# Reordering one DMA queue and moving the mLSTM set-up, its exponentials and its output gate in a hybrid decoder step on one core

## The reference, cut to what matters

```python
z = h @ w_in                                   # columns shared out to three mixers
# A) GLA: S_t = diag(a_t) S_{t-1} + k_t^T v_t, o_t = q_t S_t, chunk by chunk
# B) NSA attention: compressed, selected and window branch; the sample tokens
#    read cache_nsa_kv[page_table], compressed by a small MLP
# C) mLSTM, chunk by chunk, with a carried matrix state C:
dmat = where(causal, fcum[t] - fcum[s] + i[s], -inf)
qk   = einsum('bhtd,bhsd->bhts', q, k) * exp(dmat - m_t)
num  = einsum('bhts,bhse->bhte', qk, v) + w_state * einsum('bhtd,bhde->bhte', q, C)
C    = w_carry * C + einsum('bhs,bhsd,bhse->bhde', w_last, k, v)
o_m  = sigmoid(mo) * (rmsnorm(h_m, g) + ml_skip * u_act)   # output gate and skip
x = x + concat([o_g, o_n, o_m]) @ w_out
x = x + relu(rmsnorm(x) @ w_up)**2 @ w_down
```

## Time and profile before

| what | us |
|---|---|
| median of 3 runs | 1873.37 (1870.58 to 1886.39) |
| the profiled execution | 1873.04 |
| its span | 1871.0 (PE busy 1743.5) |
| `gla_and_gather` | 660.4 to 877.6 (217.2; PE busy 194.7, granted clock 0.94) |
| `mlstm_prompt` | 877.6 to 932.3 (54.7; PE busy 41.7, granted clock 0.67) |
| `decode_steps` | 932.3 to 965.5 (33.2; PE busy 22.2) |
| `decode_tail` | 965.5 to 1014.3 (48.8; PE busy 23.9) |
| `mix_and_mixer` | 1014.3 to 1871.0 (856.7; PE busy 837.7, granted clock 0.99) |

### The profile page before, as it was taken

How to read it: one execution, slowest core, us unless ns; L and a number is a source line. 1 busy time by engine, 2 the same in 40 slices (tenths; PEclk the granted TensorE clock), 3 DMA queues, 4 the chain that set the end, 5 groups by cost and what they waited for, 6 DMA issues and landing times. The chain is left out here.

```text
span 1871.0 us, 32344 instructions
## 1 busy us (share of the span) xinstructions
PE 1743.5 (93%) x12895; PEld 1620.8 (87%) x12895; DVE 1052.0 (56%) x1876; ACT 632.0 (34%) x1141; POOL 175.2 (9%) x205
## 2 busy tenths in 40 slices
PE   6999999979999978998865899999999999999998
PEld 6999999968888766786732899999999999999998
DVE  6372683258777755665566666444444444444445
ACT  6523331047555544443342344111112111111111
POOL 1000000022222242223111100000000000000000
PEclk7999999969999989999676999999999999999999
DMA  7741264250000165665566562111111111111102
GB/s 187 115 106 34 64 174 147 91 158 24 14 2 1 46 217 180 230 233 185 119 124 224 155 190 69 46 45 45 45 45 45 45 45 45 45 45 45 45 23 91
DMA packets 180898, 177.18 MB, mean 95 GB/s; under 512 B 51564, under 2 KB 163268, under 8 KB 177140
## 3 DMA queue, kind: packets, MB, share of 16 engines
q1 hardware_dynamic: 173924, 132.92, 25.2%
q0 software_dynamic: 2304, 33.56, 4.7%
q10 hardware_dynamic: 4560, 9.18, 1.8%
HBM read 139.60 MB, written 40.23 MB: 96 GB/s over the span
## 5 line engine op out<-in xcount | busy, mean ns | idle before, releaser
L59 PE MATMUL pm<-hH,wuH 128*128 128x344 f32 x768 | 246.3, 321 | 0.0
L61 PE MATMUL pm<-hH,wuL 128*128 128x344 f32 x768 | 245.0, 319 | 0.0
L60 PE MATMUL pm<-hL,wuH 128*128 128x344 f32 x768 | 245.0, 319 | 0.0
L59 PE MATMUL pm<-hidH,weights 128*128 128x344 f32 x720 | 230.7, 320 | 0.0
L60 PE MATMUL pm<-hidL,weights 128*128 128x344 f32 x720 | 230.2, 320 | 0.0
L61 PE MATMUL pm<-hidH,weights 128*128 128x344 f32 x720 | 230.0, 319 | 0.0
L59 PE MATMUL pz<-hH,winH 128*128 128x344 f32 x600 | 200.1, 334 | 1.6 <-DVE hL L845 1.6
L60 PE MATMUL pz<-hL,winH 128*128 128x344 f32 x600 | 194.1, 323 | 0.0
L61 PE MATMUL pz<-hH,winL 128*128 128x344 f32 x600 | 194.0, 323 | 0.0
L3302 DVE SCALAR_TENSOR_TENSOR act<-pm,onat 128x344 f32<-128x344 f32 x96 | 49.3, 515 | 239.7 <-PE pm L61 239.3
L3313 DVE TENSOR_TENSOR onat<-pm,onat 128x344 f32<-128x344 f32 x256 | 128.9, 513 | 68.9 <-PE pm L61 68.9
(11 more groups left out here) (610 smaller groups left out, 3501.1 us busy)
## 6 DMA issues: line engine op xcount, KB each, us to landing
uact<-in_w_up_dram SPq DMA_DIRECT2D x15, 1024.0 KB, 6.9
hs<-in_w_down_dram SPq DMA_DIRECT2D x15, 1024.0 KB
raw<-in_w_in_dram SPq DMA_DIRECT2D x24, 512.0 KB, 3.8
hold<-vS_scratch SPq DMA_DIRECT2D x8, 1024.0 KB, 14.4
wo<-in_w_out_dram SPq DMA_DIRECT2D x12, 512.0 KB
act<-in_w_out_dram SPq DMA_DIRECT2D x12, 512.0 KB, 5.2
zT_scratch<-zb ACTq DMA_DIRECT2D x8, 516.0 KB, 2.6
hold<-in_x_prompt_dram SPq DMA_DIRECT2D x8, 512.0 KB, 3.8
```

The source lines that it names most:

```text
L59: nc.tensor.matmul(out, wH, mH, start=start and k == 0, stop=False)
L60: nc.tensor.matmul(out, wH, mL, start=False, stop=False)
L61: last = nc.tensor.matmul(out, wL, mH, start=False, stop=stop and k == n - 1)
```

## The change

In `attend_prompt` a few buffers are allocated in another order, and SP's loads of queries and keys are reordered (the wait for the late part of z stands before keys part 4, after four query tiles and not three).

In `gla_and_gather` SP's queue goes by halves, and the small loads are spread over iterations 1 to 5. After the last gather POOL makes the masks of the next stage in a buffer that the page rows no longer need, and ACT and DVE make the rounded copies and the low part of the gates at n = 9 and n = 11 of the last iteration.

In `mlstm_prompt` the set-up is gone, `scores` is split into `decays` and `products`, `decays` runs two chunks ahead, the Sigmoid of `mo` stands after the exponential of chunk 3, and POOL's product and the warming Exp are gone.

In `decode_steps` SP loads `gains`, `skip` and `g2` after the store of `mo`. In `decode_tail` ACT multiplies `uact` by `skip`. In `mix_and_mixer` the sum with `uact` comes first and the product with `mo` after it, in one piece.

```diff
@@ attend_prompt, SP @@
-                for n in range(NQS - 1):
+                for n in range(len(KEY_PARTS) - 2):
                     load_q(n)
                     load_keys(n)
-                for n in range(NQS - 1, len(KEY_PARTS) - 1):
-                    load_keys(n)
+                for n in range(len(KEY_PARTS) - 2, NQS):
+                    load_q(n)
                 sp.wait_ge(keep["late_z"], 16 * 3)
-                for n in range(NQS - 1, TQ):
+                load_keys(len(KEY_PARTS) - 2)
+                for n in range(NQS, TQ):
                     load_q(n)
@@ gla_and_gather, SP (keep_values(s, half): the wait for the gather and the vS store;
   store_scores(s, half): the wait for the copied scores and four stores) @@
                     if 1 <= s < NCH - 1:
                         sp.wait_ge(og_done, s)
                         load_z(s + 1)
-                    for half in range(2):
-                        ... (the vS store)
-                    for half in range(2):
-                        ... (four stores of the scores)
-                    if s == 1:
-                        load_small_steps(sp, io, at, small_in)
+                    keep_values(s, 0)
+                    if s:
+                        store_scores(s - 1, 1)
+                    keep_values(s, 1)
+                    store_scores(s, 0)
+                    if 1 <= s <= 5:
+                        load_small_steps(sp, io, at, small_in, s - 1)
+                store_scores(NS - 1, 1)
@@ load_small_steps: part 0 = qkd and the four loads of head 0, parts 1 to 3 = the four
   loads of heads 1 to 3, part 4 = the two loads of gbd @@
@@ gla_and_gather, POOL, after the last gather @@
+                pool.wait_ge(f_done, NFILL * (NS - 1) + 6)
+                pool.wait_ge(v_stored[0], 16 * NS)
+                nc.gpsimd.memset(spread[:, :, :], 0.0).then_inc(pages_over, 1)
...
+                nc.gpsimd.affine_select(out=maskT[:, :, :], ...).then_inc(ml_masks, 1)
@@ gla_and_gather, ACT @@
+                        if n == 9 and it == NCH - 1:
+                            act.wait_ge(pages_over, 1)
+                            nc.scalar.activation(gates_r[:, :], R[0:64, :], ACT.Copy).then_inc(gates_high, 1)
+                            nc.scalar.activation(ident_m[:, :], ident[:, :], ACT.Copy)
+                        if n == 11 and it == NCH - 1:
+                            act.wait_ge(ml_spread, 1)
+                            nc.scalar.activation(spread_r[:, :, :], spread[:, :, :], ACT.Copy)
+                            act.wait_ge(ml_masks, 1)
+                            nc.scalar.activation(maskT_r[:, :, :], maskT[:, :, :], ACT.Copy)
@@ gla_and_gather, DVE @@
+                        if n == 11 and it == NCH - 1:
+                            dve.wait_ge(gates_high, 1)
+                            nc.vector.tensor_tensor(gates_r[32:36, :], R[0:4, :], gates_r[0:4, :].bitcast(F32), ALU.subtract)
@@ mlstm_prompt, POOL @@
-                (the memsets and affine_selects of sel127, spread, maskT)
                 constants_of_steps(nc, pool, keep, at, laid)
-                pool.wait_ge(mo_ready, 1)
-                for hp in range(HP):
-                    nc.gpsimd.tensor_tensor(uact[:, hp, :], uact[:, hp, :], at["mo"][:, hp * TT:(hp + 1) * TT], ALU.mult)
@@ mlstm_prompt, PE (decays = L2186 to L2192, products = L2193 to L2200) @@
-                scores(0)
+                decays(0)
+                products(0)
+                nc.tensor.matmul(pc[:, 0:P], sel127[:, :], ...).then_inc(wc_done, 1)
+                decays(1)
                 for c in range(NCH):
                     ... (pd(c))
                     if c + 1 < NCH:
-                        scores(c + 1)
+                        products(c + 1)
+                    if c + 2 < NCH:
+                        decays(c + 2)
                     ... (pn(c), pa(c))
@@ mlstm_prompt, ACT @@
                 for c in range(NCH):
+                    if c == 1:
+                        act.wait_ge(wc_done, 1)
+                        ... (the copy wcb, before at the stage's start)
                     ... (four Exp)
-                act.wait_ge(mo_in, 16)
-                nc.scalar.activation(at["mo"], at["mo"], ACT.Sigmoid).then_inc(mo_ready, 1)
-                nc.scalar.activation(warm[:, :], keep["eps"][0:1, :], ACT.Exp)
+                    if c == 3:
+                        act.wait_ge(mo_in, 16)
+                        nc.scalar.activation(at["mo"], at["mo"], ACT.Sigmoid)
@@ decode_steps, SP, after the store of mo (removed from decode_tail's SP) @@
+                (two loads of gains for each half, one of skip, one of g2)
@@ decode_tail, ACT, after the squares sqh @@
+                act.wait_ge(gains_in, 16 * 6)
+                for hp in range(HP):
+                    nc.scalar.activation(keep["uact"][:, hp, :], keep["uact"][:, hp, :], ACT.Copy, scale=skip[:, hp:hp + 1])
@@ mix_and_mixer, DVE, build(i) @@
-                    last = nc.vector.scalar_tensor_tensor(out=tmp[:, :, 0:n], in0=mls, scalar=gains[:, 1:2], in1=mo[:, :, at],
-                                                          op0=ALU.mult, op1=ALU.mult)
+                    last = nc.vector.scalar_tensor_tensor(out=tmp[:, :, 0:n], in0=mls, scalar=gains[:, 1:2], in1=uact[:, :, at],
+                                                          op0=ALU.mult, op1=ALU.add)
                     nc.vector.drain()
-                    for hp in range(HP):
-                        last = nc.vector.scalar_tensor_tensor(out=mixc[:, i % 2, 2 + hp, 0:n], in0=uact[:, hp, at], scalar=skip[:, hp:hp + 1],
-                                                              in1=tmp[:, hp, 0:n], op0=ALU.mult, op1=ALU.add)
-                    last.then_inc(mixc_ready, 1)
+                    nc.vector.tensor_tensor(mixc[:, i % 2, 2:4, 0:n], tmp[:, :, 0:n], mo[:, :, at], ALU.mult).then_inc(mixc_ready, 1)
```

More of the change, by code:

```diff
@@ L1608, in gla_and_gather @@
         sem = semaphores(nc, ctx, "gla", (at["gathered0"],))
+        with ExitStack() as after:
+            ml = lambda n, s, d=F32: after.enter_context(nc.sbuf_tensor(n, s, d))
+            at.update({"sel127": ml("sel127", [P, P]), "maskT_r": ml("maskT_r", [P, 4, P], F32R), "ident_m": ml("ident_m", [P, P], F32R),
+                       "spread_r": ml("spread_r", [64, 4, P], F32R), "gates_r": ml("gates_r", [64, T], F32R)})
+            spread, maskT = ml("spread", [64, 4, P]), ml("maskT", [P, 4, P])
+        sel127, maskT_r, ident_m, spread_r, gates_r = (at[n] for n in ("sel127", "maskT_r", "ident_m", "spread_r", "gates_r"))
+        R = keep["rows"]
+        sb("pages_kept", [P, 8 * 512])
         spare = keep["rows_nat"][:, :, :].rearrange("p i c -> p (i c)")
@@ L1670, in load_w1, with keep_values, store_scores @@
                                      io["w1S"].rearrange("p (j r w e) -> p j r w e", j=2, r=16, w=2)[:, j, at, :, :]).then_inc(w_in[half], 16)
+                def keep_values(s, half):
+                    sp.wait_ge(gathered[half], 16 * (s + 1))
+                    sp.dma_start(io["vS"][s, :, half * 8:half * 8 + 8, :].rearrange("p r (h d) -> p r h d", h=2),
+                                 kv[half][:, :, 3, :, :]).then_inc(v_stored[half], 16)
+                def store_scores(s, half):
+                    sp.wait_ge(sc_kept, 2 * s + half + 1)
+                    for u in range(4):
+                        sp.dma_start(sS[s * 8:s * 8 + 8, half, :, u, :], sst[32 * u:32 * u + 8, half, :].rearrange("h (f p) -> h f p", f=2)
+                                     ).then_inc(sc_stored[half], 16)
                 load_z(0)
@@ L2043, in place_small_steps, with load_small_steps @@
             "gf": sb("gfd", [P, HP, NS]), "gb": sb("gbd", [P, 2, HP])}
-def load_small_steps(sp, io, at, loads):
+def load_small_steps(sp, io, at, loads, part):
     zT = io["zT"]
-    sp.dma_start(at["qk"][:, :, :], zT[GQ:GQ + 4 * P, T:TT].rearrange("(j p) s -> p j s", p=P)).then_inc(loads, 16)
-    for h in range(4):
+    if part == 0:
+        sp.dma_start(at["qk"][:, :, :], zT[GQ:GQ + 4 * P, T:TT].rearrange("(j p) s -> p j s", p=P)).then_inc(loads, 16)
+    for h in ((part,) if part < 4 else ()):
         rws, hp = slice((h % 2) * 64, (h % 2) * 64 + 64), h // 2
@@ L2055, in load_small_steps @@
         sp.dma_start(at["gf"][rws, hp, :], zT[MF + h:MF + h + 1, T:TT].broadcast_to([64, NS])).then_inc(loads, 16)
-    for h2 in range(2):
+    for h2 in (range(2) if part == 4 else ()):
         sp.dma_start(at["gb"][h2 * 64:h2 * 64 + 64, :, :],
@@ L2192, in scores, with products @@
                     last.then_inc(pw_done, 1)
+                def products(c):
                     if c:
@@ L2304, in decode_steps @@
         mt, C, stored = at["mt"], at["C"], at["sample_out"]
+        gains, skip, g2, gains_in = keep["gains"], keep["skip"], keep["g2"], at["gains_in"]
         qbd, qbm = sb("qbd", [P, HP, NS, 2]), sb("qbm", [P, HP, NS, 2])
@@ L2345, in _ @@
```

(10 more changed lines are left out.)

82 lines of the change are left out of this document (24 added, 58 removed).

## The result

The changed kernel takes 1861.55 us in the median of 13 runs (1857.01 to 1869.50); the kernel before, timed beside it, 1875.04 (13 runs). The ratio is 0.9928, with a 95% interval of 0.9911 to 0.9945: 0.7% faster. The forecast was 1847 us, in a range of 1835 to 1860, so the gain is about half of what was forecast and the time lies 1.6 us above the range.

What follows compares the result with a forecast made beforehand. PE, busy 1,744 of 1,871 us, was taken as the bound, so only its idle or half-rate time could earn; −14.4 + 6.0 + 0.4 − 16.7 − 1.0 = −25.7 gave 1847 us, range 1835 to 1860.

Steps and rivals of the forecast that it cites:

- The −14.4 for the burst: GLA stage: spreading SP's 19 small loads removes one long iteration's idle time and half-rate work, −14.4 us.
- The +6.0 for the small groups: GLA stage: four groups of small loads each delay a gather by 1.5 us, +6.0 us (bounds 0 and 12.4).
- The DVE subtraction (+0.4): GLA stage: DVE's 1.21 us subtraction stands before the last merges and costs between 0 and 1.2, taken as +0.4 us.
- start to first `pdm`: mLSTM stage: `decays(0)` begins at once, without waiting for masks, 4.2 us to the first `pdm`, −5.9 us.
- seven intervals: mLSTM stage: from first to eighth `pdm`, two intervals of 6.2 and five of 3.45, 29.7 for 36.8, −7.1 us.
- from the eighth `pdm` to the end: mLSTM stage: POOL's tail goes, −3.8 us, and the Sigmoid among the exponentials costs +0.1 us.
- how many intervals run at half rate?: mLSTM stage: PE's clock falls at the barrier and two intervals run at half rate, between none and four.
- The Sigmoid in the middle (+0.1): mLSTM stage: Sigmoid and two table loads, 4.5 us between exponentials, which ACT catches up; 0 to 3, taken as +0.1 us.
- Two chunks ahead: mLSTM stage: earlier input to the exponential removes PE's wait at full rate, an interval of 3.45 in place of 3.83 us.
- decode_steps and decode_tail (0): Decode stages: SP's six moved issues (3.6 us) and ACT's two products with `skip` fall into idle time, 0.
- The mix (−1.0): `mix_and_mixer`: one product replaces two pieces, −0.46 us for each build, bounds 0 and −4.1, taken as −1.0 us.
- the clock's staying down: Rival, mLSTM stage: the clock stays down as long as before, four intervals, +5.5 us, time 1853; chance 0.20.

Runs made afterwards that it cites:

- e4: The kernel before with only the 19 small loads of the GLA stage spread over iterations 1 to 5, behind the score stores: 1864.61 us, ratio 0.9927.
- e5: The changed kernel with `decays(c+2)` put directly before `products(c+1)`, still two chunks ahead: 1857.83 us, ratio 0.9892.
- e12: The changed kernel itself once more, unaltered: 1859.50 us, ratio 0.9922.
- e1: The changed kernel with seven transposes of the identity after PE's last GLA output, in front of the barrier: 1853.73 us, ratio 0.9885.
- e3: The changed kernel with all 19 small loads in one run in GLA iteration 1 again: 1869.97 us, ratio 0.9961.
- e7: The changed kernel, its order kept, with 13 transposes of the identity around PE's last GLA output: 1847.07 us, ratio 0.9810.
- e2: The changed kernel with `decays(c+1)` directly before `products(c+1)`, one chunk ahead as in the kernel before: 1852.30 us, ratio 0.9866.
- e9: The changed kernel with 13 transposes around the last GLA output and `decays(c+1)` directly before `products(c+1)`, one chunk ahead: 1854.43 us, ratio 0.9896.
- e10: The program of e6 with the Sigmoid of `mo` moved after the last exponential: 1846.29 us, ratio 0.9861.
- e11: The program of e6 once more, in more rounds: 1847.89 us, ratio 0.9872.
- e15: The program of e5 once more: 1853.87 us, ratio 0.9883.
- e8: The changed kernel with one more matmul of 512 columns, result unused, in every mLSTM chunk but the first: 1849.17 us, ratio 0.9865.
- e14: The changed kernel with `decays(c+2)` directly before `products(c+1)` and an added matmul in every chunk but the first: 1855.48 us, ratio 0.9901.
- e16: The program of e8 once more: 1856.75 us, ratio 0.9901.
- e6: The changed kernel with `decays(c+2)` directly before `products(c+1)` and 13 transposes around PE's last GLA output: 1837.34 us, ratio 0.9801.
- e13: The program of e6 with an added matmul in every chunk but the first and two more before the first `pdm`: 1844.10 us, ratio 0.9831.

## Why the prediction was wrong, point by point

**The GLA stage: right in what goes, wrong in what comes.** The −14.4 for the burst is what was measured (−14.0 with everything). The +6.0 for the small groups (1.5 us for each of four) was mis-sized: it is 0 in the changed kernel. The place was right, beside the gather of half 0; the price was not. I took it from a gather in the middle of the burst (14.3 us to landing), and here the loads begin behind the gather, which then lands after 8.9 to 9.1 us, 0.3 to 0.5 us over the 8.6 that I had reckoned with and within the 2.6 to spare. The price that I had in mind is paid in e4, where the loads begin ahead of a gather: its groups cost 14.4 − 5.7 = 8.7 us, in a place that I did not name (the gather of half 1). The Trainium skill ("DMA: Bandwidth & Descriptors", section "Issuing engines are not separate DMA queues") has all transfers interleave on the same 16 engines, by which the upper bound, 12.4 us, had been weighed; e4's landings of 13.4 to 14.5 us agree with it. The upper bound that I drew from it does not hold in the changed kernel, where the landings are 8.9 to 9.1 us.

**The DVE subtraction (+0.4):** not visible; the stage is 14.0 shorter where −14.4 alone would be 0.4 more, but its length in the eight traces with this stage's code unchanged runs from 202.5 to 203.9.

**The mLSTM stage: here it failed.** By its terms, from the two timelines:

| term | forecast | measured |
|---|---|---|
| start to first `pdm` | −5.9 | −5.1 (4.9 us in place of 10.1) |
| seven intervals | −7.1 | +8.1 (44.9 in place of 36.8) |
| from the eighth `pdm` to the end | −3.7 | −2.9 (5.0 in place of 7.9) |

The step that failed is "how many intervals run at half rate?": I took two, with four as the upper bound, and all seven did. The bound was four because the kernel before had four, and I argued that more work from the start could only bring the clock back sooner. The runs show otherwise. The second step that failed is smaller and was in the diff to be seen: I priced an interval at half rate as unchanged, 6.2 us, "running `decays` two ahead is worth nothing there", but the new neighbours cost 0.5 us in each of the six intervals that still hold a `decays`, 2.9 us together; the seventh is 1.3 us shorter than 6.2, for the `decays` that went in front. e5, with both neighbours put back, has 6.17 us. I had weighed each matmul by its own duration and not by its neighbours.

What holds the clock down? Of the traces in which it fell at the start of the stage, the changed order without added work has five (the changed kernel, e12, e1, e3, e7), and in none did it come back within 49 us of the stage's start, when the recurrence was in its last chunk or over. With `decays` directly before `products` there are eight, with the masks made early or late: it came back after 18 to 36 us in seven (before, e2, e5, e9, e10, e11, e15), and only after 55 us in one, e4 (its stage: 59.9 us). With a matmul added to each chunk it came back after 27, 19 and 19 us in all three (e8, e14, e16). From the first `pdm` to the clock's return PE is busy without a gap in all of these stretches, so "busy" does not tell them apart. Nor do the transfers of the stage: the clock came back while the DMA engines were at a share of 1.4 (e5, 886 to 896), and stayed at 0.50 long after they had gone quiet (0.01 in the changed kernel from 895 to 917). That the changed order delays the return is therefore well supported in the traces, and that one more matmul in each chunk brings the clock back in the same order is what e8 and e16 show in one execution each. How it is decided stays open, and so does why one program (e6 and e11, or e4 beside the kernel before) goes one way in one execution and another in the next. The share of executions in which the clock comes back isn't known: only the traced ones show it, and the medians of e5, e14, e15 and e16 (1854 to 1858) lie nearer the changed kernel's (1860 to 1862) than their traces would suggest.

**The Sigmoid in the middle (+0.1):** right, by e6's trace, as long as `decays` is two chunks ahead (e2's pause of 2.16 us). The Trainium skill ("ScalarE: Activation LUTs", section "What ACT_TABLE_LOAD costs") has a drain of some 1.4 us besides the load of 1.28 at each change of table; here e6's load begins at 876.35 and the Sigmoid at 877.64, so no drain is seen.

**Two chunks ahead:** 3.45 us forecast at full rate, 3.31 measured in e6, with no wait of PE. In the changed kernel it earned nothing, since no interval ran at full rate.

**decode_steps and decode_tail (0):** −0.6 and +1.2. In decode_tail the read of `win_rows` from `sS_scratch` held DVE 2.80 us where it had been 0.85:

```profile
963.98 2.28 DVE L2799 TENSOR_REDUCE bm<-win_rows 64x32 f32<-64x2048 f32 x1 [2.80 <-DMA win_rows<-sS_scratch]
```

It starts 12.6 us after the stage's start, before 10.4. That the six loads moved ahead of decode_steps' stores are the cause wasn't tried, and the difference itself is within the scatter: the same code took 47.1 to 50.6 us for this stage in the other traces. The two products by `skip` on ACT took 2.2 us of idle time, as forecast (5.91 us of idle time remain of 7.79).

**The mix (−1.0):** the one product takes 0.43 us in the chain of work, where the two pieces took 0.62 to 0.70:

```profile
1033.32 0.43 DVE act L3268
```

The stage as a whole took between 851.6 and 858.6 us in the traces of this study and 856.7 before, so a microsecond can't be found in it.

**The chances:** the clock's staying down had 0.20, at 1853 us, and that is the rival nearest to what happened; but it was bounded at four intervals. With all seven, 44.9 us as measured against the forecast's 2 × 6.2 + 5 × 3.45 = 29.7, the sum is 15 us higher, and with the groups at 0, 6 lower: 1857. What the start and the end of the stage fell short by, 0.8 us each, and the mix's missing gain bring it near the measured 1861.55. The range should have held the case in which the clock does not come back at all.

**A faster version.** The changed kernel with `decays(c+2)` directly before `products(c+1)` and 13 transposes around the last GLA output (e6 and e11) takes 1844.4 us in the median of ten runs, 0.9801 and 0.9872 of the kernel before in its two studies. It is the best that was measured, beside e13 (1844.1); as the clock decides between its 1833 and its 1858 us, the median of another ten runs may differ.

## What to carry to other kernels

Where a stage is bound by TensorE, ask for its clock first, and give a forecast of it a branch in which the clock does not come back within the stage: the same matmuls took 34 or 55 us here in two orders, and 34 or 42 us in one and the same program. Before matmuls are reordered, see which neighbours overlap; the sum of their durations alone does not show it. When transfers are moved in a queue, redraw the queue's whole timeline after the change, with the stands that have gone, and see what the moved transfers are issued ahead of: four small loads that began ahead of a gather held it up as much as nineteen had, and the same loads begun behind a gather cost nothing.

## What the runs showed of the hardware that was not expected

- TensorE stayed at 0.50 for over 50 us while it was busy without a pause (864.0 to 916.5), and one more matmul of 512 columns in each chunk brought it back to 1.00 after 27 and 19 us (e8, e16, one trace each).
- The order of the same matmuls is worth 0.5 us in a chunk at half rate, 6.17 against 6.66 us: two sets of 64-row matmuls overlap when they are issued side by side (2.0 against 2.2 us), and the group behind `pdm` starts after 0.83 or 1.10 us, by what it is.
- A gather of 2 MB landed after 8.9 to 9.1 us with a group of small loads begun 0.3 to 1.1 us behind it (the changed kernel), and after 13.4 to 14.5 us with a group begun 1.2 to 2.2 us ahead of it (e4).
- One and the same program ran its mLSTM stage in 34.0 us and in 42.5 us (e6, e11, on two chips). The difference lies in the granted clock, 0.97 and 0.68 in the stage.
